# Second expert stage of a two-layer kernel: when its first weights are sent, and from where its first two gathers read

## The chip, the cores and the metric

The kernel runs on one core of a Trainium2 chip. A core has a matrix engine (TensorE, PE in the profile; its weight loads are PEld), a vector engine (VectorE, DVE), a scalar engine (ScalarE, ACT), GpSimd (POOL) and a queue that issues most DMAs (SyncE, SP or SPq). The metric is the device time of one execution in microseconds. The kernel before takes 781.3 us, the median of 3 runs from 780.98 to 781.67.

## The reference

A sequence of 16 meta tokens and 256 tokens of 1024 features goes through two layers. Each has a mixer (layer 0: two recurrences side by side; layer 1: gated linear attention, `gla_mix`, in chunks of 64 tokens) and then 32 experts with a hierarchical router. Everything is f32. The change touches only the second layer's experts and the final norm:

```python
def rms_norm(x, gain):
    y = x * lax.rsqrt(jnp.mean(x * x, axis=-1, keepdims=True) + 1e-6)
    return y * gain

def hier_moe(h, ...):                      # h: 272 x 1024
    g_idx = argmax(h @ w_group + b_group)  # 1 of 4 groups
    # of the 8 experts of that group the 2 with the largest logits,
    # weights: softmax over the two, times the group's probability
    for e in range(32):                    # w_gate, w_up: 1024 x 256, w_down: 256 x 1024
        hid = silu(h @ w_gate[e]) * (h @ w_up[e])
        y = y + (hid @ w_down[e]) * combine[:, e:e + 1]

h = h + gla_mix(rms_norm(h, o_norm) @ o_w_in) @ o_w_out
h = h + hier_moe(rms_norm(h, m_norm[1]), ...)
return rms_norm(h[:, 16:], final_norm)
```

## The kernel before

**Memory.** `M` is one tile of 128 partitions by 45312 floats, used again and again. In the expert stages it holds four slots of 8192 floats (`slots`, 4 MB each), from columns 0, 8192, 16384 and 37120, the normalised rows `xn` (24576 to 27648), the one-hots `R` and weighted one-hots `RW[0]`, `RW[1]`, the gathered tokens `xgT`, and the outputs `yst`. `H` holds the residual rows: `H[:, 0]` and `H[:, 1]` the 256 tokens, `H[:, 2]` the meta tokens, which layer 1's experts don't need any more.

**The expert stage.** `experts(y)` exists once for each engine, y being the layer. Experts go in 8 turns of four, q = 0 to 7, and each turn has three units of weights of 4 MB: unit 3q is gate, 3q + 1 up, 3q + 2 down. `UNIT_SLOT` gives each unit its slot; in layer 1 units 0 to 11 take slots 0, 1, 2, 3 in turn. The first half of a gate or up unit (`0:D`) holds contraction blocks k = 0 to 3, the second (`D:2*D`) k = 4 to 7. SyncE issues the DMAs in the order of units, each behind a wait for the slot's last reader: in layer 1 unit 0 behind `mix_part` 1 (the first of four chunks of the mixer's output, L395), unit 1 behind `mix_part` 4 (L397), unit 3 in two halves behind `res_done` 9 and 11 (the output projection's blocks, L399, L412), unit 4 behind `half_done` 3 (the first half of unit 0's gate is used, L429), unit 5 in halves behind `half_done` 4 and the end of unit 1, and from unit 6 on each behind the end of the unit that had the slot (L433). Unit 4's first half is set aside elsewhere (`set_aside`, semaphore `ld_half`). Unit 6 takes slot 2 after unit 2, the down weights of q = 0.

**A turn on TensorE** (L1576 to L1633): gate (L1554), then `combined` of the turn before (L1512), up (L1554), the weighted one-hots turned back (L1505), the gather for the next turn (L1497, blocks k = 0 to 3), the transposes of hid (L1617), down (L1630), and the rest of the gather (k = 4 to 7). A gather is a matmul for each k and each of two token tiles n, with `xn[:, n, k, :]` (128 adjacent floats) stationary and `R[:, n, :]` moving; `gathered` on VectorE applies the gain `gm`. In q = 0 the gather is `first_gather` (L1411), interleaved with the router's matmuls and the halves of gate and up, so that it goes on while the second tile's tokens are still being routed. Each f32 matmul stands in the trace as two records, each with its weight load.

**Normalisation.** ScalarE squares and sums the rows (L544, L807, L814), VectorE inverts the root (L1990), and ScalarE's `normed(n)` (L803) writes `xn[:, n]`, reading H with a step of 8 floats (`"p (d k) -> p k d"`) and writing adjacent ones, times `rs`. `xn_set` counts these. `first_onehot` and `onehot` on VectorE make `R` from the slot numbers `RM`, `weighted` makes `RW` from `R`; `R_set` and `RW_set` count them. `link` makes an engine wait for its own last instruction.

**The end.** `fnb` is the gain of the final norm spread over all partitions, loaded by a DMA of 0.5 MB into `H[:, 2]` during layer 1's projections (L509, after the group g = 8). The last accumulations, the norm and three output DMAs follow q = 7. `keep_busy` is a filler of matmuls on ones. `oproj` counts the projections of layer 1 (22 in all), `qk_set` the scaled keys and queries of its 6 levels.

## Time and profile before

| | |
|---|---|
| median of 3 runs | 781.3 us (780.98 to 781.67) |
| span of the profiled execution | 778.7 us, mean granted TensorE clock 0.975 |
| PE, DVE, ACT, POOL busy | 92%, 42%, 26%, 4% of the span |
| DMA | 242.14 MB, mean 311 GB/s; 420 to 424 GB/s in the full slices |
| chain that ended last | PE 60%, DMA 15%, DVE 4% |
| second expert stage, from its first weight load to the last output | 522.3 to 778.7 us |

The profile is one execution; its times count from the span's start. The runs' time lies 2.6 us above the span. The page cuts the span into 40 slices of 19.5 us. A timeline row gives start, length, engine, line, operation, what it writes and reads, shapes and, in brackets, the engine's idle time before it and what ended that. Rows of one kind in sequence are merged, with their count.

### The profile page before, as it was taken

How to read it: one execution, taken by the hardware profiler on the slowest of the kernel's cores; microseconds unless marked ns; L12 is line 12 of the kernel's file. 1: busy time of each engine (PE TensorE's matmuls, PEld its weight loads, DVE VectorE, ACT ScalarE, POOL GpSimd, SP SyncE). 2: the span in 40 equal slices, each digit the busy share in tenths (PEclk: the TensorE clock that was granted, in tenths of full speed). 3: DMA queues.
4: the chain of work that ended last, by engine and by line, in shares of the span. 5: the costliest groups of instructions: out<-in, count | busy, mean ns of one | idle time of the engine just before them, and what ended most of it. 6: DMA issues, size and time to landing. Idle time of an engine off the chain costs nothing.

```text
span 778.7 us, 16693 instructions
## 1 busy us (share of the span) xinstructions
PE 718.9 (92%) x7444; PEld 459.4 (59%) x7444; DVE 324.4 (42%) x688; ACT 205.9 (26%) x414; POOL 31.7 (4%) x99
## 2 busy tenths in 40 slices
PE   9999999999989998999999999999998976786696
PEld 7778787658646464564548746884764543343342
DVE  7476977535353422333235065541445321221222
ACT  2574577215100000000041454630510000000003
POOL 7006000000000000000000000000000000000000
PEclk9999999999999997999999999999999998989999
DMA  8644113499999999999999731019999999999995
GB/s 265 201 107 142 56 57 112 161 418 417 386 420 419 420 421 421 417 419 422 411 339 370 231 107 58 2 36 424 421 391 421 422 420 419 421 422 422 420 406 199
DMA packets 72757, 242.14 MB, mean 311 GB/s; under 512 B 9894, under 2 KB 37660, under 8 KB 52588
## 3 DMA queue, kind: packets, MB, share of 16 engines
q1 hardware_dynamic: 72476, 240.52, 79.0%
q8 instruction: 59, 0.97, 0.5%
q10 hardware_dynamic: 208, 0.54, 0.2%
q14 instruction: 14, 0.11, 0.0%
HBM read 240.00 MB, written 1.05 MB: 310 GB/s over the span
## 4 chain that ended last, share of the span: by engine, by line
PE 60%; DMA 15%; DVE 4%; issue 1%; SPq 1%; ACT 0%; ACTq 0%
PE ps L1554 11%; PE ps L1874 10%; PE ps L1396 7%; PE ps L1497 6%; DMA M<-in_m_w_gate_dram 6%; PE ps L1630 5%; PE ps L1512 5%; DMA M<-in_m_w_up_dram 4%; DMA M<-in_m_w_down_dram 4%; PE ps L1035 2%; DVE H L2488 1%; PE ps L1411 1%; PE ps L1696 1%; PE ps L1768 1%; PE ps L1505 1%
## 5 line engine op out<-in xcount | busy, mean ns | idle before, releaser
L1554 PE MATMUL ps<-M 128*32 128x256 f32 x2016 | 124.2, 396 | 18.4 <-DMA M<-in_m_w_gate_dram 11.4
L1554 PEld LDWEIGHTS ps<-M 128*32 128x32 f32 x2016 | 66.7, 114 | 74.7 <-issue 16.9
L1089 PE MATMUL ps<-M 128*128 128x272 f32 x352 | 85.3, 397 | 0.1
L1874 PE MATMUL ps<-M 128*128 128x256 f32 (+2 forms) x288 | 79.9, 434 | 0.0
L1497 PEld LDWEIGHTS ps<-M 128*128 128x128 f32 x608 | 71.5, 192 | 12.3 <-issue 11.8
L1497 PE MATMUL ps<-M 128*128 128x128 f32 x608 | 76.9, 278 | 0.0
L1089 PEld LDWEIGHTS ps<-M 128*128 128x128 f32 x352 | 65.6, 190 | 15.4 <-issue 1.7
L1630 PE MATMUL ps<-M 128*32 128x512 f32 x448 | 58.7, 671 | 15.5 <-DMA M<-in_m_w_down_dram 15.5
L1512 PE MATMUL ps<-M 128*128 128x512 f32 (+1 forms) x120 | 62.8, 647 | 5.3 <-DVE H L2488 5.3
L1874 PEld LDWEIGHTS ps<-M 128*128 128x128 f32 x288 | 53.7, 190 | 22.6 <-issue 15.6
L2485 DVE TENSOR_TENSOR H<-H,ps 128x512 f32<-128x512 f32 x60 | 41.2, 687 | 57.5 <-PE ps L1512 57.3
L1396 PE MATMUL ps<-M 128*128 128x512 f32 (+1 forms) x160 | 57.5, 512 | 0.0
L2464 DVE TENSOR_TENSOR M<-ps,gm 128x512 f32<-128x512 f32 x28 | 19.4, 692 | 59.7 <-PE ps L1497 59.7
L1512 PEld LDWEIGHTS ps<-M 128*128 128x128 f32 (+1 forms) x120 | 19.9, 194 | 40.7 <-DVE H L2485 18.1
L1630 PEld LDWEIGHTS ps<-M 128*32 128x32 f32 x448 | 15.7, 120 | 47.7 <-issue 46.5
L831 ACT ACTIVATE M<-ps 128x256 f32<-128x256 f32 x16 | 6.1, 383 | 140.7 <-PE ps L1554 140.7
L1396 PEld LDWEIGHTS ps<-M 128*128 128x128 f32 x160 | 29.6, 190 | 23.0 <-issue 21.5
L833 ACT ACTIVATE M<-ps 128x272 f32<-128x272 f32 x16 | 6.4, 397 | 127.1 <-PE ps L1505 127.1
L2540 DVE COPY M<-ps 128x512 f32<-128x512 f32 x14 | 9.7, 692 | 64.2 <-PE ps L1630 64.2
L839 ACT ACTIVATE M<-ps 128x512 f32<-128x512 f32 x16 | 9.6, 597 | 62.2 <-PE ps L1630 57.3
L2488 DVE TENSOR_TENSOR H<-H,ps 16x256 f32<-16x256 f32 x32 | 13.3, 414 | 29.7 <-PE ps L1514 29.4
L1021 POOL TENSOR_SCALAR M<-M,rs 128x512 f32<-128x512 f32 x1 | 1.6, 1566 | 548.0 <-DVE rs L1990 548.0
(462 smaller groups left out, 843.6 us busy)
## 6 DMA issues: line engine op xcount, KB each, us to landing
M<-in_m_w_gate_dram SPq DMA_DIRECT2D x31, 2048.0 KB, 19.0
M<-in_m_w_down_dram SPq DMA_DIRECT2D x24, 2048.0 KB, 22.8
M<-in_m_w_up_dram SPq DMA_DIRECT2D x24, 2048.0 KB, 21.6
M<-in_o_w_in_dram SPq DMA_DIRECT2D x12, 1024.0 KB, 9.5
M<-in_e_w_in_dram SPq DMA_DIRECT2D x11, 1024.0 KB, 6.7
M<-in_m_w_down_dram SPq DMA_DIRECT2D x10, 1024.0 KB, 18.1
M<-in_m_w_up_dram SPq DMA_DIRECT2D x9, 1024.0 KB, 17.9
M<-in_m_w_down_dram SPq DMA_DIRECT2D x4, 1536.0 KB, 13.3
```

Source lines behind the costliest of these rows:

```text
L1035: pe.matmul(ps[:, bank, :].rearrange("p (a c) -> p a c", a=4), ones[:, :], ones[:, :].unsqueeze(1).to_broadcast([P, 4, P]), start=True, st ...
L1089: ins = pe.matmul(ps[:, n % 4, 0:T], wringE[:, (n // 2) % 4, k, (n % 2) * P:(n % 2) * P + P], (xnE if n else xuE)[:, k], start=(k == 0), s ...
L1396: ins = pe.matmul(res, mixT[:, k, TOK[n]], w_out, start=(k == 0), stop=(k == 7))
L1497: ins = pe.matmul(ps[:, 1 + k // 4, (k % 4) * P:(k % 4) * P + P], xn[:, n, k, :], R[:, n, :], start=(n == 0), stop=(n == nt - 1))
L1512: return pe.matmul(ps[:, bank, :], rt_[:, TOK[n]], ys[:, 512 * hf:512 * hf + 512], start=True, stop=True)
L1554: ins = pe.matmul(ps[32 * e:32 * e + 32, 3 * x, 0:FF], xgT[q % 2][:, k, 32 * e:32 * e + 32], w, start=(k == 0), stop=(k == KD - 1))
L1630: ins = pe.matmul(ps[r, 4 + hf, :], hidT[:, k, r], dn_w[UNIT_SLOT[y][u]][:, e, k, 512 * hf:512 * hf + 512], start=(k == 0), stop=(k == 1))
L1874: ins = pe.matmul(ps[rows, unit % 4, 0:n], lhs(k), rhs(k), start=(k == 0), stop=(k == KD - 1))
L2464: return tt(xgT[q % 2][:, 4 * b:4 * b + 4], ps[:, 1 + b, :].rearrange("p (k t) -> p k t", k=4), gm[:, y, 4 * b:4 * b + 4].unsqueeze(2).to_ ...
L2485: return tt(H[:, n, c], H[:, n, c], ps[:, 6 + j % 2, :], ALU.add)
L2488: ins = tt(H[0:META, 2, c], H[0:META, 2, c], ps[32 * g:32 * g + META, 6 + j % 2, 0:256], ALU.add)
L2540: v.tensor_copy(yst[q % 2][:, 512:1024], ps[:, 5, :]).then_inc(s("yd"), 1)
```

## The change

**Loads.** In layer 1, unit 0 is sent when the projections are done (`oproj` 22) instead of with `mix_part` 1: its experts 2 and 3 whole, and of experts 0 and 1 the second half. Their first halves go where `xn[:, 0:2]` lies, after `mix_part` 4. The room left in slot 0 takes the second halves of unit 4's experts 0 and 1 at once. Unit 1's experts 0 and 1 are sent behind `qk_set` 6, the rest behind `mix_part` 4. Half an expert's down weights of unit 5 are loaded into `H[:, 2]` during the projections.

**Gathers.** In layer 1 the gathers for q = 0 and q = 1 read `H` itself with a step of 8 floats (`rows_at`), and the factor `rs` goes into the one-hot: `first_onehot` and `onehot(1)` write the plain one-hot into `RW[0]` and `RW[1]` and multiply it into `R`. `normed(0)` and `normed(1)` come in q = 0, before the silu and after the copy of hidT, and VectorE's first accumulation waits for them, since it changes `H`.

**Final norm.** The gain is loaded as 8 rows of 128 into `before`. At the head of q = 4 and q = 5 TensorE spreads four rows each over all partitions into PSUM bank 3, and ScalarE copies them to `fnb`, now at column 26624. Up of that turn waits for the copy.

Cut to its core (`...` marks what is left out):

```diff
-        fnb = H[:, 2, :]
+        first_half = [[], [xn[:, n].rearrange("p k t -> p (k t)") for n in range(2)]]
+        fnb = at(26624, D)
+        fn_rows = before[0:KD, :]
+        down_half = H[:, 2, :]
...
                         if y == 0:
                             sp.wait_ge(s("oc_set"), NC)
                         else:
-                            sp.wait_ge(s("mix_part"), 1)
+                            sp.wait_ge(s("oproj"), sum(O_UNITS))
+                            sp.dma_start(slots[j][:, 2:4, :], gate[:, 2:4, :]).then_inc(s(f"ld_s{j}"), 16)
+                            sp.dma_start(slots[j][:, 0:2, D:2 * D], gate[:, 0:2, D:2 * D]).then_inc(s(f"ld_s{j}"), 16)
+                            sp.dma_start(slots[j][:, 0:2, 0:D], up[:, 4:6, D:2 * D]).then_inc(s("ld_half"), 16)
+                            continue
                     elif u == 1 and y == 1:
+                        sp.wait_ge(s("qk_set"), 6)
+                        sp.dma_start(slots[j][:, 0:2, :], up[:, 0:2, :]).then_inc(s(f"ld_s{j}"), 16)
                         sp.wait_ge(s("mix_part"), 4)
+                        sp.dma_start(xn[:, 0:2].rearrange("p n k t -> p n (k t)"), gate[:, 0:2, 0:D]).then_inc(s("ld_s0"), 16)
+                        sp.dma_start(slots[j][:, 2:4, :], up[:, 2:4, :]).then_inc(s(f"ld_s{j}"), 16)
+                        continue
...
                         elif u == 4:
-                            sp.dma_start(slots[j][:, 2 * h:2 * h + 2, 0:D], src[:, 4 + 2 * h:6 + 2 * h, D:2 * D]) \
-                                .then_inc(s(f"ld_s{j}"), 16)
+                            if h == 1:
+                                sp.dma_start(slots[j][:, 2:4, 0:D], src[:, 6:8, D:2 * D]).then_inc(s(f"ld_s{j}"), 16)
                         elif u == 5:
                             if h == 1:
                                 wait_through(UNIT_PREV[y][u])
-                            sp.dma_start(slots[j][:, :, D * h:D * h + D], src[:, 4:8, D * h:D * h + D]).then_inc(s(f"ld_s{j}"), 16)
+                            sp.dma_start(slots[j][:, 1 - h:4, D * h:D * h + D], src[:, 5 - h:8, D * h:D * h + D]).then_inc(s(f"ld_s{j}"), 16)
...
                 if g == 8:
-                    sp.dma_start(fnb, a["final_norm"].rearrange("(o d) -> o d", o=1).broadcast_to([P, D])).then_inc(s("ld_wr"), 16)
+                    sp.dma_start(fn_rows, a["final_norm"].rearrange("(k c) -> k c", c=P)).then_inc(s("ld_gn"), 16)
+                    sp.dma_start(down_half, a["m_w_down"][1, 4].rearrange("(p k) d -> p (k d)", k=2)[:, 0:D]).then_inc(s("ld_wr"), 16)
...
-                act.wait_ge(s("rec"), (5, 10)[y])
-                normed(0)
-                if nt == 3:
+                if y == 0:
+                    act.wait_ge(s("rec"), (5, 10)[y])
+                    normed(0)
                     normed(2)
...
-                act.wait_ge(s("rec"), (6, 11)[y])
-                normed(1)
+                if y == 0:
+                    act.wait_ge(s("rec"), (6, 11)[y])
+                    normed(1)
...
                 for q in range(NQ):
                     n = NQ * y + q
+                    if q == 0 and y == 1:
+                        act.wait_ge(s("half_done"), 2 * y + 1)
+                        act.wait_ge(s("rec"), (6, 11)[y])
+                        normed(0)
+                    if y == 1 and q in (4, 5):
+                        act.wait_ge(s("vec_tr"), q + 3)
+                        nc.scalar.activation(fnb[:, 512 * q - 2048:512 * q - 1536], ps[:, 3, :], ACT.Copy).then_inc(s("rb_set"), 1)
...
+                    if q == 0 and y == 1:
+                        normed(1)
...
+            def rows_at(n, k):
+                return H[:, n, :].rearrange("p (d k) -> p k d", k=KD)[:, k, :]
...
-                        ins = pe.matmul(ps[:, GATHER_BANK[k // 2], (k % 2) * P:(k % 2) * P + P], xn[:, n, k, :], R[:, n, :],
+                        ins = pe.matmul(ps[:, GATHER_BANK[k // 2], (k % 2) * P:(k % 2) * P + P], rows_at(n, k) if y == 1 else xn[:, n, k, :], R[:, n, :],
...
-                pe.wait_ge(s("xn_set"), (2, 4)[y])
+                if y == 0:
+                    pe.wait_ge(s("xn_set"), (2, 4)[y])
...
-                            ins = pe.matmul(ps[:, 1 + k // 4, (k % 4) * P:(k % 4) * P + P], xn[:, n, k, :], R[:, n, :],
+                            from_rows = rows_at(n, k) if first and y == 1 else xn[:, n, k, :]
+                            ins = pe.matmul(ps[:, 1 + k // 4, (k % 4) * P:(k % 4) * P + P], from_rows, R[:, n, :],
...
+                            elif u == 0 and k < KD // 2 and e < len(first_half[y]):
+                                w = first_half[y][e][:, FF * k:FF * k + FF]
...
+                    if y == 1 and q in (4, 5):
+                        pe.wait_ge(s("ld_gn"), 80)
+                        for k in range(4 * q - 16, 4 * q - 12):
+                            ins = pe.matmul(ps[:, 3, (k % 4) * P:(k % 4) * P + P], ident[0:KD, k:k + 1].to_broadcast([KD, P]), fn_rows,
+                                            start=True, stop=True)
+                        ins.then_inc(s("vec_tr"), 1)
...
+                            if y == 1 and q in (4, 5):
+                                pe.wait_ge(s("rb_set"), q + 3)
                             half_gu(3 * q + 1, q, 1, range(4 if q == 0 and y == 1 else 0, KD))
...
-                        gather(ks=range(0, 2))
+                        if y == 1 and q == 1:
+                            pe.wait_ge(s("xn_set"), (3, 5)[y])
+                        gather(ks=range(0, 2), first=(q == 0))
...
-                        gather(s("g_done"), range(2, 4))
+                        gather(s("g_done"), range(2, 4), q == 0)
...
-                                ins = pe.matmul(ps[r, 4 + hf, :], hidT[:, k, r],
-                                                dn_w[UNIT_SLOT[y][u]][:, e, k, 512 * hf:512 * hf + 512], start=(k == 0), stop=(k == 1))
+                                w = dn_w[UNIT_SLOT[y][u]][:, e, k, 512 * hf:512 * hf + 512]
+                                if y == 1 and u == 5 and e == 0 and k == 0:
+                                    w = down_half[:, 512 * hf:512 * hf + 512]
+                                ins = pe.matmul(ps[r, 4 + hf, :], hidT[:, k, r], w, start=(k == 0), stop=(k == 1))
                         ins.then_inc(s("dn_done"), 1)
-                    gather(ks=range(4, KD)).then_inc(s("g_done"), 1)
+                    gather(ks=range(4, KD), first=(q == 0)).then_inc(s("g_done"), 1)
...
+                    if y == 0:
+                        return tt(R[:, t_].rearrange("p t (e c) -> p t e c", e=4),
+                                  iota[:, 1:CAP + 1].unsqueeze(1).unsqueeze(1).to_broadcast([P, m, 4, CAP]),
+                                  RM[:, t_, 0:4].unsqueeze(3).to_broadcast([P, m, 4, CAP]), ALU.is_equal).then_inc(s("R_set"), 1)
+                    link(tt(RW[0][:, t_].rearrange("p t (e c) -> p t e c", e=4),
+                            iota[:, 1:CAP + 1].unsqueeze(1).unsqueeze(1).to_broadcast([P, m, 4, CAP]),
+                            RM[:, t_, 0:4].unsqueeze(3).to_broadcast([P, m, 4, CAP]), ALU.is_equal))
+                    tt(R[:, t_], RW[0][:, t_], wide3(rs[:, ri], P, t_, m), ALU.mult).then_inc(s("R_set"), 1)
...
+                    hot = RW[q] if y == 1 and q == 1 else R
+                    made = tt(by_slot(hot), iota[:, 1:CAP + 1].unsqueeze(1).unsqueeze(1).to_broadcast([P, nt, 4, CAP]),
+                              RM[:, t_, 4 * q:4 * q + 4].unsqueeze(3).to_broadcast([P, nt, 4, CAP]), ALU.is_equal)
+                    if hot is not R:
+                        link(made)
+                        made = tt(R[:, t_], hot[:, t_], wide3(rs[:, ri], P), ALU.mult)
+                    made.then_inc(s("R_set"), 1)
                     v.wait_ge(s("R_set"), (NQ + 1) * y + q + 2)
...
-                    tt(by_slot(RW[q % 2]), by_slot(R), WT[:, t_, 4 * q:4 * q + 4].unsqueeze(3).to_broadcast([P, nt, 4, CAP]),
+                    tt(by_slot(RW[q % 2]), by_slot(RW[q] if y == 1 and q < 2 else R), WT[:, t_, 4 * q:4 * q + 4].unsqueeze(3).to_broadcast([P, nt, 4, CAP]),
...
+                    if y == 1 and q == 0:
+                        v.wait_ge(s("xn_set"), (3, 5)[y])
...
-                    v.wait_ge(s("ld_wr"), 176)
+                    v.wait_ge(s("rb_set"), 8)
```

## Rows read from the trace of the kernel before

**Rows 1.** The page: share and rate of the DMA engines in 40 slices.
```profile
DMA  8644113499999999999999731019999999999995
GB/s 265 201 107 142 56 57 112 161 418 417 386 420 419 420 421 421 417 419 422 411 339 370 231 107 58 2 36 424 421 391 421 422 420 419 421 422 422 420 406 199
```

**Rows 2.** Timeline of PE, 604 to 779 us: start, length, engine, line, operation, idle before.
```profile
621.47 2.05 PE L1497 MATMUL ps<-M 128*128 128x128 f32 x16
627.12 5.35 PE L1554 MATMUL ps<-M 128*32 128x256 f32 x64 [3.60 <-DMA M<-in_m_w_gate_dram]
...
656.93 5.35 PE L1554 MATMUL ps<-M 128*32 128x256 f32 x64 [2.52 <-DMA M<-in_m_w_gate_dram]
```

**Rows 3.** The chain of work that ended last, in order of time: start, length.
```profile
737.97 6.27 PE ps L1630 x32
```

**Rows 4.** Timeline of the SyncE queue: when it issued the weight loads.
```profile
522.30 0.88 SPq L468 DMA_DIRECT2D M<-in_m_w_gate_dram  x2
529.24 0.88 SPq L468 DMA_DIRECT2D M<-in_m_w_up_dram  x2
...
568.08 0.88 SPq L461 DMA_DIRECT2D M<-in_m_w_up_dram  x2
...
580.87 0.88 SPq L468 DMA_DIRECT2D M<-in_m_w_gate_dram  x2
586.44 0.88 SPq L468 DMA_DIRECT2D M<-in_m_w_up_dram  x2
```

**Rows 5.** DMA issues, windows 522:523 and 580:582 us: KB each, median us to landing.
```profile
M<-in_m_w_gate_dram SPq DMA_DIRECT2D x2, 2048.0 KB, 10.5
...
M<-in_m_w_gate_dram SPq DMA_DIRECT2D x2, 2048.0 KB, 13.7
```

**Rows 6.** Timeline of PE, 511 to 582 us.
```profile
511.73 1.89 PE L1874 MATMUL ps<-M 128*128 128x256 f32 x8
...
552.02 1.87 PE L1431 MATMUL ps<-wrc,M 128*128 128x36 f32 x16
...
560.76 1.58 PE L1411 MATMUL ps<-M 128*128 128x128 f32 x12
...
564.00 1.93 PE L1411 MATMUL ps<-M 128*128 128x128 f32 x12
566.09 3.66 PE L1554 MATMUL ps<-M 128*32 128x256 f32 x64 [0.16 <-DVE M L2469]
569.68 1.16 PE L1411 MATMUL ps<-M 128*128 128x128 f32 x8
...
575.05 1.06 PE L1497 MATMUL ps<-M 128*128 128x128 f32 x8
...
577.17 3.64 PE L1630 MATMUL ps<-M 128*32 128x512 f32 x32
```

**Rows 7.** Timeline of DVE, 560 to 574 us: the first one-hots and the second.
```profile
560.33 0.29 DVE L2405 TENSOR_TENSOR M<-iota,M 128x128 f32<-128x128 f32 x1
...
564.37 0.29 DVE L2405 TENSOR_TENSOR M<-iota,M 128x128 f32<-128x128 f32 x1
...
573.64 0.43 DVE L2455 TENSOR_TENSOR M<-iota,M 128x256 f32<-128x256 f32 x1
```

**Rows 8.** Lines 803 and 544 (ACT): shortest/median/longest in ns, first and last start.
```profile
L803 ACT ACTIVATE M<-H,rs x5: 2135/2157/2160, 180.2 to 560.1; 128x1024 f32<-128x1024 f32 x5
...
L544 ACT ACTIVATE M<-H x5: 1042/1050/1057, 5.4 to 548.4; 128x1024 bf16<-128x1024 f32 x4, 16x1024 bf16<-16x1024 f32 x1
```

**Rows 9.** Timeline of ACT in q = 0: the silu.
```profile
572.91 0.38 ACT L831 ACTIVATE M<-ps 128x256 f32<-128x256 f32 x1 [3.86 <-PE ps L1554]
```

**Rows 10.** Timeline of PE's weight loads, the first gather of tile 0.
```profile
560.74 1.41 PEld L1411 LDWEIGHTS ps<-M 128*128 128x128 f32 x12 [0.20 <-issue]
```

**Rows 11.** Lines 1617 (step of 2 floats) and 1505 (adjacent): weight loads, in ns.
```profile
L1617 PEld LDWEIGHTS ps<-ident,M x32: 194/199/218, 204.0 to 761.7; 128*128 128x128 f32 x32
...
L1505 PEld LDWEIGHTS ps<-ident,M x32: 186/190/192, 574.5 to 761.3; 128*128 128x128 f32 x32
```

More of the change, by code:

```diff
@@ L1529, in loaded @@
                     j = UNIT_SLOT[y][u]
-                    pe.wait_ge(s(f"ld_s{j}"), 32 * (FIRST_LAYER[j] * y + UNIT_TURN[y][u] + 1))
+                    more = 0
+                    if (y, u) == (1, 0):
+                        more += 16
+                    pe.wait_ge(s(f"ld_s{j}"), 32 * (FIRST_LAYER[j] * y + UNIT_TURN[y][u] + 1) + more)
                     if y == 0 and u == 1:
```

16 lines of the change are left out of this document (7 added, 9 removed).

## The prediction, made before the changed kernel was run

> **What bounds the kernel now.** I read the page first, for the stage that matters. The DMA engines move about 420 GB/s, all they give here, through nearly every slice of the second expert stage, and fall to 2 and 36 GB/s in the two slices before it [rows 1]. The change works on that border, so the time is in the chain behind it. The PE timeline shows that from the fourth turn of the stage (q = 3) TensorE stands and waits for weights: 3.60 us before gate at 627.12, 2.52 us at 656.93 [rows 2]. A unit of 4 MB takes (656.93 − 627.12)/3 = 9.94 us. The last such wait ends at 737.97; behind it comes only TensorE's own tail, whose first piece took 6.27 us [rows 3]. So the end moves with the stream of weights, one for one.
>
> The stream goes by the SyncE queue, in order. It starts at 522.30. Unit 4 is issued at 568.08, when half of unit 0's gate is used up. Unit 6 is the one that matters. It is issued at 580.87, when the down matmuls of q = 0 (577.17 + 3.64) have ended and slot 2 is free [rows 4, 6]. With an empty queue two loads of 2 MB land 10.5 us after their issue (median, 522.30); unit 6's land after 13.7 us [rows 5]. So 3.2 us of older work stood ahead of unit 6. That is the reserve: **the stream can move forward by 3.2 us at most, unless TensorE ends q = 0 sooner.** Behind it each slot comes free well before the stream wants it: unit 7 is issued at 586.44, and its data flow only when unit 6 has landed, at 627.12 − 3 × 9.94 = 597.3 [rows 2, 4]; the distance grows with each later unit. Nothing later holds the stream.
>
> **Part 1, earlier loads.** Unit 0, a quarter of unit 4 and half of unit 1 no longer wait for the first mixed chunk (522.30) but for the end of the projections, 511.73 + 1.89 = 513.6 [rows 4, 6]: 8.7 us sooner. They are 6 MB, 15 us of stream, to 529 or 530, where the wait for the fourth chunk ends (529.24) [rows 4]. The 0.5 MB of down for unit 5 that comes during the projections, in the place of the norm's broadcast of 0.5 MB, takes 1.2 us more out. Taken alone that is near 9 us. It is lost: the stream then runs dry before 547 to 559, where the output matmuls free slot 3, and again before units 4 and 5, which are still released by TensorE inside q = 0, and stands empty when unit 6 comes. What is left is the 3.2 us, less any delay of q = 0. The issues themselves take 0.4 us of SyncE each, under the stream.
>
> **Part 2, normalisation on ScalarE.** Two passes of 2.16 us leave the way to the router. TensorE did not wait for them: the gathers of tile 0 began at 560.76 and those of tile 1 at 564.8, each just behind its one-hot of VectorE (560.33 + 0.29 = 560.62, 564.37 + 0.29 = 564.66) [rows 6, 7], and the second pass had ended at 560.1 + 2.16 = 562.3 [rows 8]. Gain 0. They come back in q = 0: normed(0) where ScalarE idles 3.86 us before the silu [rows 9], normed(1) beside the down matmuls. Cost 0; without this cover 2.2 us. VectorE's new wait in accumulated(0) has the accumulations and the table of q = 1 behind it, and is met some 7 us early (normed(1) ends near 580, the first combine near 587).
>
> **Part 3, scaled one-hots.** Each first_onehot gets a linked multiplication of 128 columns, as long as the comparison, 0.29 us, and about 0.04 us for the link; onehot(1) one of 256 columns, 0.43 us [rows 7]. The first lies on the path (+0.3 us). The second lies on it too (+0.3 us) if the gathers cost what they did, and is hidden if they become slower; the third has TensorE's turn_back and first gather beside it. Together +0.3 to +0.7 us.
>
> **Part 4, gathers from the residual rows.** This decides. The stationary operand was xn[:, n, k, :], 128 adjacent floats; now it is H with a step of 8 floats, 32 bytes. There are 16 such matmuls in the first gather and 16 in the second, each of two records. The instructions are as many as before; the question is how long a weight load takes. Two rows say that the load is the limit even now: 12 records in 1.41 us, (1.41 − 0.19)/11 = 0.11 us apart, where 0.19 us is one load alone, and the logits with a moving side of only 36 columns are no faster: 1.87 us for 16, about 0.11 us each [rows 6, 10]. Nothing hides a longer load.
>
> No row shows a weight load with this step. Bounds from the nearest: ScalarE reads the same rows of H with the same step of 8 in 2157 ns (L803) and adjacent ones in 1050 ns (L544): +1.08 ns per element, +138 ns for 128 [rows 8]. The weight load of hid with a step of 2 took 199 ns against 190 ns for adjacent ones [rows 11], +9 ns: the lower end, and a load may even be free of any cost (0). Zero stands for a TensorE that does not mind the step. I take **+0.12 us a record**: ScalarE's row is the only one with this very step and these very rows, less a little, since part of its difference may be the f32 output.
>
> The Trainium skill bears both ways. "Advanced Engine Details and Errata", section SBUF Cachelines, has lines of 16 bytes and wants two hits in a line for full rate; ScalarE's 2157 against 1050 ns agrees. By it the 199 ns of step 2 mean (110 + 9)/64 = 1.86 ns a line, and step 8 an estimated 128 × 1.86 = 238 ns against 110, +0.13 us: the sum below with half a microsecond more. "TensorE: Matmul & The Clock Gate", section LDWEIGHTS, gives the load as columns/1.2 ns, 107 ns, with no word on the step; the 0.11 us above agrees, and by that rule alone the load would not change and the first rival would hold.
>
> **The sum.** Ahead of the end of q = 0's down stand 12 + 4 + 16 records of the first gather and 16 of the second [rows 6]: 48 × 0.12 = 5.8 us. Add 0.3 for the first multiplication. Take off the short waits of TensorE in this stretch that are now filled (0.11 before 564.80, 0.16 before 566.09, 0.5 before 570.91): −0.7. So unit 6 is issued 5.4 us later, at 586.3, to an empty queue, and lands 5.4 − 3.2 = 2.2 us later than before. The last 16 strided records follow q = 0's down, and TensorE reaches q = 3 at 623.52 [rows 2] + 5.4 + 1.9 = 630.8 against weights at 629.3; the 1.5 us are made good at once, since gate took 5.35 us behind a wait and takes 3.66 us without one [rows 2, 6], and up waits for its weights anyway. End: **+2.2 us**, span 778.7 + 2.2 = 780.9. The median of the runs is 2.6 us above the span, which I keep: 783.5.
>
> **Part 5, final norm by TensorE.** Four matmuls of 128 columns ahead of gate in q = 4 and q = 5, about 0.9 us each time, and a copy of 0.6 us on ScalarE. TensorE waits 2.52 us for weights at that very place [rows 2]: 0. Without the cover 1.8 us. The wait on rb_set before up has gate's 3.66 us ahead of it: 0. The last stage waits for rb_set where it waited for the old load, both done by then.
>
> **Rivals.** (a) *The step is free for TensorE.* Then only part 3 delays q = 0, +0.7 us, and the stream gains 3.2 − 0.7 = 2.5 us: 778.8. For it: the load with step 2 is almost as fast, and no row shows TensorE suffer from a step. Against: ScalarE's row, and that the load already sets the pace. It decides if the extra is under 0.03 us a record. This is the case on the other side. (b) *The step costs 0.03 to 0.08 us*: 48 of them less the covers give 1.2 to 3.4 us of delay, −1.8 to +0.7, mostly within 0.2%: about 781. (c) *The earlier start reaches the end*, −9 us, 772: it needs unit 6 issued before 575, and that issue belongs to TensorE. I give it nothing but the edge. (d) *The tail*: down at 737.97 took 6.27 us, where the same matmuls took 3.64 us in q = 0 [rows 3, 6]. A shift of the whole stage can put it elsewhere: −2 to +1 us in any case. It widens the range and has no chance of its own.
>
> **How the numbers follow.** Forecast 0.58, with +0.09 to +0.14 us a record: +0.8 to +3.2 us, 782.1 to 784.5, and 1 more for the tail. Rival (a) 0.31, (b) 0.10, (c) 0.01. About 0.2% (1.6 us) is what a measurement of this kernel can tell from no change. Slower: 0.50 of the forecast and 0.02 of (b). Same: 0.08 of the forecast, 0.04 of (a), 0.06 of (b). Faster: 0.27 of (a), 0.02 of (b), 0.01 of (c). The range must hold both sides: from 778.2, just below (a), to 785.2. The forecast's own is 781.8 to 785.2.
>
> **What would show it.** The weight loads of first_gather with about 315 ns where they had 190 (right) or still 190 (rival a). Unit 6 issued near 586 (right) or 581.5 (a). The DMA engines idle just before unit 6: in both. No wait of TensorE for gate at q = 3. The wait for weights before gate at q = 4 and 5 shorter by 0.9 us, its end unmoved by it. Wrong would be the whole reasoning if unit 6 still found older loads ahead of it, or if the first gathers began later than 561.2 for another reason.

## The result, and the profile of the changed kernel

| | before | changed |
|---|---|---|
| median of the runs compared | 781.3 us (779.88 to 783.17, 5 runs) | 788.8 us (785.47 to 789.97, 5 runs) |
| ratio, 95% interval | 1 | 1.0081 (1.0061 to 1.0100) |
| the same again, in a later series | 781.43 us (23 runs) | 786.15 us (785.40 to 787.59, 6 runs); 1.0061 (1.0041 to 1.0081) |
| span of the profiled execution | 778.7 us | 783.7 us, granted clock 0.972 |

The change costs 0.6 to 0.8%. All 11 runs of the changed kernel together have a median of 787.3 us, 5.9 above the 781.4 of before. The prediction said slower by 2.2 us, range 778.2 to 785.2; the direction was right, the size was not.

The page's DMA rows of the changed kernel, in the same 40 slices as [rows 1]:

```profile
DMA  8644113499999999999999531079869999999995
GB/s 262 201 109 139 55 57 110 186 417 415 387 420 419 419 422 421 418 420 421 406 339 370 173 108 56 2 289 385 345 238 379 421 420 420 421 420 421 421 405 196
```

The empty slice ahead of the stage is filled (36 became 289 GB/s), and the rate falls behind it: 385, 345 and 238 where [rows 1] has 424, 421 and 391. The stream was moved forward and then stood.

The queue of SyncE, 512 to 592 us (start, length, what it issued), against [rows 4]:

```profile
513.63 0.37 SPq L399 DMA_DIRECT2D M<-in_m_w_gate_dram  x1
...
530.61 0.37 SPq L407 DMA_DIRECT2D M<-in_m_w_gate_dram  x1
531.02 0.47 SPq L408 DMA_DIRECT2D M<-in_m_w_up_dram  x1
...
572.69 0.37 SPq L474 DMA_DIRECT2D M<-in_m_w_up_dram  x1
574.42 6.06 SPq L478 DMA_DIRECT2D M<-in_m_w_down_dram  x2
588.34 0.88 SPq L480 DMA_DIRECT2D M<-in_m_w_gate_dram  x2
```

Unit 0 leaves 8.7 us sooner. But SyncE's wait for the fourth mixed chunk (`mix_part` 4; called the fourth chunk's wait below, its end being the issue behind it) ends at 530.61 instead of 529.24, unit 4 is released at 572.69 instead of 568.08, and unit 6 at 588.34 instead of 580.87: 7.47 us later. It meets a queue that is all but empty (107 GB/s from 588 to 590 us) and takes 10.5 us to land, where [rows 5] has 13.7.

PE, 518 to 593 us, against [rows 6] (start, length, line, shapes, in brackets the idle time before and what ended it):

```profile
520.31 0.42 PE L1974 MATMUL ps<-M,ones 128*32 128x64 f32 x12
521.84 0.31 PE L1974 MATMUL ps<-M,ones 128*32 128x64 f32 x4 [1.11 <-issue]
...
562.44 3.24 PE L1437 MATMUL ps<-M,H 128*128 128x128 f32 x12 [0.42 <-DVE M L2460]
565.48 2.14 PE L1058 MATMUL ps<-ones 128*128 128x512 f32 x4
...
567.56 3.21 PE L1437 MATMUL ps<-M,H 128*128 128x128 f32 x12
570.69 3.66 PE L1589 MATMUL ps<-M 128*32 128x256 f32 x64
574.28 2.17 PE L1437 MATMUL ps<-M,H 128*128 128x128 f32 x8
...
580.53 2.07 PE L1525 MATMUL ps<-M,H 128*128 128x128 f32 x8
...
584.64 3.64 PE L1679 MATMUL ps<-M 128*32 128x512 f32 x32
588.21 4.08 PE L1525 MATMUL ps<-M,H 128*128 128x128 f32 x16
```

The gathers of 12 and 8 records take about twice what they took. And there is a stall of 1.11 us in the mixer, at 520.73, that no row of before has; the trace puts it down to issue, that is, to nothing that it shows. The weight loads of the strided gathers (shortest/median/longest in ns; `ps<-M,H` are those of layer 1, `ps<-M` the adjacent ones of layer 0):

```profile
L1437 PEld LDWEIGHTS ps<-M x48: 186/192/192, 187.6 to 196.0; 128*128 128x128 f32 x48
L1437 PEld LDWEIGHTS ps<-M,H x32: 312/336/338, 562.4 to 575.9; 128*128 128x128 f32 x32
...
L1525 PEld LDWEIGHTS ps<-M,H x32: 312/335/338, 580.4 to 591.8; 128*128 128x128 f32 x32
```

PE, 652 to 743 us, the waits for weights, against [rows 2, 3], and the spreading of the final norm (L1619):

```profile
652.06 4.94 PE L1679 MATMUL ps<-M 128*32 128x512 f32 x32 [3.70 <-DMA M<-in_m_w_down_dram]
...
658.91 1.15 PE L1619 MATMUL ps<-before,ident 8*128 8x128 f32 x8
661.91 5.15 PE L1589 MATMUL ps<-M 128*32 128x256 f32 x64 [1.85 <-DMA M<-in_m_w_gate_dram]
...
742.98 5.34 PE L1679 MATMUL ps<-M 128*32 128x512 f32 x32 [3.68 <-DMA M<-in_m_w_down_dram]
```

Gate of q = 4 gets its weights at 661.91 instead of 656.93, and the last down at 742.98 instead of 737.97: 5.0 us each, as the span. The last down takes 5.34 us instead of 6.27, but the end is no sooner for it.

One measure helps in all that follows. The data of unit 11 (down of q = 3) end a wait of TensorE in every profile, at 647.09 before and 652.06 after; from there to the end of the span are 131.5 to 131.8 us in before, the changed kernel and the first four experiments alike. So **the end is unit 6's issue, plus the time until the data of unit 11 are there (six units of 4 MB, 6 to 11), plus a constant**: the middle term is 66.22 us before (580.87 to 647.09) and 63.72 after. The 2.5 us between the two are all that the stream gains, and 7.47 − 2.5 = 5.0.

### The profile page after: what moved, and what is told of

The parts are those of the page before. It is cut to its first block, busy times and chain, and to the rows that moved or that the text cites. A ratio compares the mean times of both kernels' runs of the same rounds, so it can differ in the third digit from the quotient of the medians.

```text
span 783.7 us, 16735 instructions
## 1 busy us (share of the span) xinstructions
PE 729.4 (93%) x7460; PEld 469.0 (60%) x7460; DVE 325.2 (42%) x691; ACT 206.7 (26%) x416; POOL 31.5 (4%) x99
## 4 chain that ended last, share of the span: by engine, by line
PE 59%; DMA 13%; DVE 4%; SPq 4%; issue 1%; ACT 0%; PEld 0%; PEldq 0%; ACTq 0%
PE ps L1589 11%; PE ps L1922 10%; DMA M<-in_m_w_gate_dram 7%; PE ps L1419 7%; PE ps L1525 7%; DMA M<-in_m_w_down_dram 5%; PE ps L1540 5%; PE ps L1679 4%; SPq L470 2%; PE ps L1437 2%; DVE H L2546 1%; PE ps L1058 1%; SPq L464 1%; PE ps L1816 1%; PE ps L1533 1%
## 5 line engine op out<-in xcount | busy, mean ns | idle before, releaser
L1589 PEld LDWEIGHTS ps<-M 128*32 128x32 f32 x2016 | 65.5, 114 | 67.2 <-issue 15.9
L1525 PEld LDWEIGHTS ps<-M 128*128 128x128 f32 x576 | 68.5, 194 | 11.4 <-issue 10.9
L1112 PEld LDWEIGHTS ps<-M 128*128 128x128 f32 x352 | 65.6, 190 | 15.5 <-issue 1.7
L1525 PE MATMUL ps<-M 128*128 128x128 f32 x576 | 73.6, 280 | 0.0
L1922 PEld LDWEIGHTS ps<-M 128*128 128x128 f32 x288 | 53.7, 190 | 22.6 <-issue 15.6
L1679 PEld LDWEIGHTS ps<-M 128*32 128x32 f32 x444 | 15.2, 120 | 47.2 <-issue 46.1
L1419 PEld LDWEIGHTS ps<-M 128*128 128x128 f32 x160 | 29.6, 190 | 23.0 <-issue 21.5
```

Source lines behind the costliest of these rows:

```text
L1112: ins = pe.matmul(ps[:, n % 4, 0:T], wringE[:, (n // 2) % 4, k, (n % 2) * P:(n % 2) * P + P], (xnE if n else xuE)[:, k], start=(k == 0), s ...
L1419: ins = pe.matmul(res, mixT[:, k, TOK[n]], w_out, start=(k == 0), stop=(k == 7))
L1525: ins = pe.matmul(ps[:, 1 + k // 4, (k % 4) * P:(k % 4) * P + P], from_rows, R[:, n, :], start=(n == 0), stop=(n == nt - 1))
L1589: ins = pe.matmul(ps[32 * e:32 * e + 32, 3 * x, 0:FF], xgT[q % 2][:, k, 32 * e:32 * e + 32], w, start=(k == 0), stop=(k == KD - 1))
L1679: ins = pe.matmul(ps[r, 4 + hf, :], hidT[:, k, r], w, start=(k == 0), stop=(k == 1))
L1922: ins = pe.matmul(ps[rows, unit % 4, 0:n], lhs(k), rhs(k), start=(k == 0), stop=(k == KD - 1))
```

## The experiments

The first four pull the two large parts of the change apart. They ran together (before: 781.45 us, 35 runs).

**1. The gathers read adjacent floats.** The features come in another order, so the output is another; instructions, bytes and waits are the same.

```diff
             def rows_at(n, k):
-                return H[:, n, :].rearrange("p (d k) -> p k d", k=KD)[:, k, :]
+                return H[:, n, k * P:(k + 1) * P]
```

> The changed kernel, but the first two gathers read 128 adjacent floats of H instead of every eighth. (So the features of the gathered tokens are in another order than the weights' rows, and the experts' output of q = 0 and 1 is another one; amount and order of work are the same.) Theory A, the step of 8 floats is what costs: the weight loads of the gathers fall from 336 to 192 ns, q = 0's down ends 48 x 0.144 = 6.9 us sooner than in the changed kernel, near 581.4 to 582 in its profile, unit 6 meets an empty queue and lands about 1 us sooner than in the kernel before; time 780 us, plus whatever the early loads cost in stalls (1 to 4 us): 780 to 784. Theory B, the earlier traffic or the moved passes of ScalarE are what costs and the step only adds what would be hidden: no more than 2 us are won, 787 us. Theory C, the whole loss is the step: 778.8, as the first rival of the prediction had it.

Measured: 781.83 us (779.11 to 783.93, 12 runs), ratio 0.9993 (0.9974 to 1.0012): within theory A's range, B and C are out. Unit 6 is issued at 582.96, 52.23 us behind the fourth chunk's wait instead of 57.73. That is 1 us later than theory A had it, and the queue was not empty: unit 6 took 12.0 us to land.

**2. The late start.** The early loads wait for the first mixed chunk again; the step stays.

```diff
-                            sp.wait_ge(s("oproj"), sum(O_UNITS))
+                            sp.wait_ge(s("mix_part"), 1)
...
-                        sp.wait_ge(s("qk_set"), 6)
```

> The changed kernel with one part undone: unit 0 and the first half of unit 1 wait again for the mixer's first and fourth chunk. Theory A: the queue is empty at unit 6 anyway, so nothing of the early start is lost, and the stall of 1.1 us in TensorE's issue at 520.7, which came when 6 MB of weights ran beside the mixer's end, goes: q = 0's down ends at 586.9 instead of 588.3, time 1.4 us below the changed kernel's if the stall is the same in each run, 2 to 4 us below if its other runs (spans 785.8 to 788.2 against 783.7 of the profiled one) have longer ones: 784 to 787. Theory D, the early start is worth its 3 us of reserve: 2 to 3 us slower than the changed kernel, 791.

Measured: 786.38 us (783.98 to 791.06, 12 runs), ratio 1.0057 (1.0038 to 1.0075). Unit 6 at 588.65, landing 10.4 us later. Without the early start the kernel is no slower than the changed one; theory D's 791 did not come. The stall is gone in this profile, but unit 6 is no sooner: the filler took 3.01 us instead of 2.14, at a granted clock of 0.50 (1.2 GHz) from 564 to 566 us.

**3. Both edits together.**

> Both edits of the two runs before at once: adjacent reads (another order of features, same amount of work) and the late start. What is left of the change is the scaled one-hots, normed in q = 0, the weights in xn's place, the 0.5 MB of down during the projections, and the final norm by TensorE. Theory A: q = 0's down ends at 581.5 (0.7 us late by the multiplications), the stream has 1.2 us less before unit 6, which lands 1.2 us sooner: 780 us, 1 us below the kernel before or the same. Theory B (moved passes of ScalarE cost): over 783.

Measured: 781.6 us (779.37 to 783.86, 12 runs), ratio 0.9998 (0.9980 to 1.0016). Unit 6 comes 53.89 us behind the fourth chunk's wait, 1.66 more than in experiment 1 with the same gathers. The granted clock was 0.50 from 564 to 566 us here and 1.00 there: the first twelve records took 2.07 instead of 1.60 us, the filler 3.14 instead of 1.88.

**4. The kernel before with the early start alone** (unit 0 at the end of the projections, unit 1's first half behind `qk_set` 6).

> The kernel before with one part added: unit 0 whole at the end of the projections and the first half of unit 1 behind the last keys; nothing else. Theory A: the stream before unit 6 is done early, unit 6 lands 581 + 13.2 = 594.3 instead of 597.3 if q = 0 is not delayed, 1.4 us less gain with a stall of TensorE's issue near 520: 778.4 to 780. If the runs of the changed kernel that lie 2 to 4 us above its profiled one do so by such stalls, this one shows it as well: a spread over 3 us in its runs, median 780 to 782. Theory D: -3 us, 778.3, with no stall.

Measured: 782.7 us (781.22 to 785.33, 12 runs), ratio 1.0011 (0.9996 to 1.0026). Unit 6 at 582.31, 1.44 later than before; 1.0 of that is a stall in the mixer (below). Unit 11's data come 66.18 us behind it: of the reserve nothing is used.

What follows from the four: the step accounts for nearly the whole loss (with it 786.4 to 787.3, without it 781.6 to 781.8, whatever the start). The early start is worth nothing in either company: 9 us of stream moved ahead are lost before unit 6. Nor do these medians show a price of it that is clear of the noise: what it costs the mixer is read from the profiles alone.

The next four ran together (before: 781.43 us, 23 runs).

**5. The changed kernel again,** unaltered.

> The changed kernel, nothing altered, beside the others and with a profile of its own. It settles how much of the gap between the median (+7.5 us) and the profiled execution (+5.0 us) is spread. Theory A (the profiled execution was simply a fast one): the median comes out 786 to 789, and this profile shows TensorE's stall ahead of the stage of another length than 1.11 us, with unit 6 issued 57 to 58.5 us behind the last mixed chunk as before. Rival: the median falls to about 784.5, 1.75 us above the span of 783.7 plus the usual 1 us; then 2 to 4 us of the first result were chance of one job.

Measured: 786.15 us (785.40 to 787.59, 6 runs), 2.7 us below the first median. Its profile has the same span, 783.6, unit 6 at 588.20, and the stall again, shorter:

```profile
520.92 0.42 PE L1974 MATMUL ps<-M,ones 128*32 128x64 f32 x12
522.04 0.30 PE L1974 MATMUL ps<-M,ones 128*32 128x64 f32 x4 [0.70 <-issue]
```

So of the first result's 7.5 us, 4.7 come back, and all eleven runs give 5.9. The granted clock was 0.969 to 0.973 in the first five runs and 0.970 to 0.979 in these six; whether that made the difference, no run tells.

**6. The changed kernel without the filler** between the first gather of tile 0 and the ranks of tile 1.

```diff
                 first_gather(y, range(0, 6), (0, 2)[0:2 - y])
-                if y == 1:
-                    keep_busy(2, 3)
```

> The changed kernel without the two filler matmuls (keep_busy(2, 3)) between the first gather of tile 0 and the ranks of tile 1. They took 2.14 us there, and VectorE's input to the ranks (A_set) was ready before they began, since the strided gather ended 1.7 us later than before. Theory A (everything ahead of the down matmuls of q = 0 is on the path one for one): TensorE ends q = 0 some 1.9 to 2.1 us sooner, unit 6 is issued so much sooner, and the end comes 1.9 us sooner than in the unchanged kernel of this job, about 785.5 to 786. Rival B (something else waits behind it, such as VectorE's second one-hot or a lower clock without the filler): at most 0.5 us, and the idle time of TensorE before the ranks or before the second gather grows by what the filler took.

Measured: 784.23 us (782.60 to 786.71, 12 runs), ratio 1.0030 (1.0015 to 1.0045), 1.9 us below experiment 5. Unit 6 comes 55.68 us behind the fourth chunk's wait (588.30 − 532.62) instead of 57.39 to 57.73. As theory A said. The VectorE row of the changed kernel shows how it came to lie on the path: the ranks' input was written by 565.3, and then VectorE stood for TensorE:

```profile
565.05 0.25 DVE L2437 SCALAR_TENSOR_TENSOR M<-M 128x32 bf16<-128x32 f32 x1
...
567.70 0.19 DVE L2446 SCALAR_TENSOR_TENSOR M<-ps,M 128x32 f32<-128x32 f32 x1 [2.24 <-PE ps L1516]
```

In the kernel before, the filler covered a wait of TensorE (experiment 12 shows 0.55 us of it with half the filler). The slower gather in front of it used up that wait, and the filler kept its length: the 1.7 us that the first twelve loads cost would have been hidden, had the filler given way.

**7. The kernel before with half an expert of unit 5 loaded early and the norm spread by TensorE** (`fnb`, `fn_rows`, `down_half` and what belongs to them in the diff; nothing of the gathers, one-hots or early start).

> The kernel before with only two pieces of the change: half an expert's down weights of unit 5 (0.5 MB) loaded into the meta tokens' rows during the projections in the place of the norm's broadcast, and the final norm spread by TensorE in q = 4 and q = 5. The step, the early start and the scaled one-hots are left out. Theory A (what moves the stream is only how little stands ahead of unit 6, and 0.5 MB is 1.2 us of it): unit 6 is issued at the same time as before, lands about 1.2 us sooner (reserve was 2.5 to 3.2 us), and the whole end moves by 1.2 us: 780.2, ratio 0.9985. TensorE's four small matmuls ahead of gate lie in its wait for weights: 0. Rival B (the spreading costs, or the reserve is not reached by work taken out of unit 5): 781.4 or more, ratio 1.000 or above, and the wait for weights before gate of q = 4 ends no sooner than before.

Measured: 780.58 us (779.65 to 786.06, 12 runs), ratio 0.9991 (0.9974 to 1.0007). The interval holds no change and theory A's 0.9985 both. In the profile unit 11's data came 65.95 us behind unit 6's issue instead of 66.22: a gain of 0.3 us, not 1.2. The half megabyte is gone (the load is shown with 1536 KB), but the DMA engines moved 354 GB/s from 576 to 578 us where before they moved 397. Why is open.

**8. The step as a scale.** First gather of layer 1 with steps of 1 to 8 floats, a line for each (the tokens of q = 0 hold other features):

```diff
-                        ins = pe.matmul(..., rows_at(n, k) if y == 1 else xn[:, n, k, :], ...)
...
+                        elif k == 0:
+                            ins = pe.matmul(out_, H[:, n, 0:128:1], R[:, n, :], ...)
+                        elif k == 1:
+                            ins = pe.matmul(out_, H[:, n, 0:255:2], R[:, n, :], ...)
...
+                        elif k == 7:
+                            ins = pe.matmul(out_, H[:, n, 0:1017:8], R[:, n, :], ...)
```

> The changed kernel, where the first gather of layer 1 reads its eight feature blocks from the residual rows with steps of 1, 2, 3, 4, 5, 6, 7 and 8 floats, a line of its own for each, so that each step's weight load has its own row. The tokens gathered for q = 0 hold other features than the reference wants. It measures the cost of the step. Theory A (cost by lines of 16 bytes, as ScalarE's read suggests: one line for each element from a step of 4 on): 190 ns at step 1, rising in proportion up to step 4, and level at about 335 ns from 4 to 8. Theory B (cost by bytes spanned): a straight line from 190 at step 1 to 336 at step 8, with 199 at step 2 and 250 at step 4. Theory C (32 bytes are special, and below them the load is nearly free): 190 to 210 ns for steps 1 to 7 and 336 at 8 alone.

It ran once, in 785.1 us, and its time is not compared. Weight loads of 128 x 128 f32 with steps of 1, 2, 3, 4, 5 and 8 floats, in this order (shortest/median/longest in ns):

```profile
L1441 PEld LDWEIGHTS ps<-M,H x4: 186/188/189, 562.5 to 568.9; 128*128 128x128 f32 x4
L1443 PEld LDWEIGHTS ps<-M,H x4: 196/197/198, 562.8 to 569.1; 128*128 128x128 f32 x4
L1445 PEld LDWEIGHTS ps<-M,H x4: 254/258/263, 563.0 to 569.4; 128*128 128x128 f32 x4
L1447 PEld LDWEIGHTS ps<-M,H x4: 317/324/330, 563.3 to 569.8; 128*128 128x128 f32 x4
L1449 PEld LDWEIGHTS ps<-M,H x4: 295/316/319, 563.8 to 574.0; 128*128 128x128 f32 x4
...
L1455 PEld LDWEIGHTS ps<-M,H x4: 334/335/336, 568.2 to 575.4; 128*128 128x128 f32 x4
```

Theory A, with one correction: step 2 is almost free (197), step 3 costs +70, step 4 already +136, and 5 to 8 add nothing much (316 to 335). The Trainium skill, "Advanced Engine Details and Errata", section SBUF Cachelines, has lines of 16 bytes that must be hit twice for full rate; the trace agrees: two floats of a line are the last step that is free, and from one float a line on the price is level. Theories B and C are out.

The last four ran together (before: 781.43 us, 35 runs).

**9. One megabyte early.** The kernel before; expert 0 of gate at the end of the projections, the other three with the first mixed chunk.

```diff
+                            sp.wait_ge(s("oproj"), sum(O_UNITS))
+                            sp.dma_start(slots[j][:, 0:1, :], gate[:, 0:1, :]).then_inc(s(f"ld_s{j}"), 16)
                             sp.wait_ge(s("mix_part"), 1)
+                            sp.dma_start(slots[j][:, 1:4, :], gate[:, 1:4, :]).then_inc(s(f"ld_s{j}"), 16)
+                            continue
```

> The kernel before, with 1 MB of unit 0 (expert 0 of gate) sent at the end of the projections and the other 3 MB with the first mixed chunk, as before. The early traffic then fills only 2.5 us, 514.3 to about 517, and is over when TensorE reaches the place (near 520.5 us) where it stalled 0.5 to 1.1 us in every kernel with 6 MB sent early and in none without. Theory A (the stall comes from weights in flight at that moment): no stall, the fourth mixed chunk is ready as early as before (issue of unit 1 near 529.1), unit 6 issued at 581, and the time is the one before, 781.4 within 0.6. Rival B (the stall comes from the order of the issues, or from SyncE's waits, whatever is in flight): the stall stays, 0.5 us or more, and the time is near that of the early start alone, 782.5.

Measured: 781.62 us (780.46 to 787.41, 12 runs), ratio 1.0010 (0.9992 to 1.0028), and no stall; the 16 records stand in one piece:

```profile
520.26 0.43 PE L1930 MATMUL ps<-M,ones 128*32 128x64 f32 x16
520.63 1.15 PE L1918 MATMUL ps<-M 128*64 128x64 f32 x32
```

The time from the end of the projections to the end of the fourth chunk's wait, in all profiles:

| kernel | early loads | that time, us | stall shown, us |
|---|---|---|---|
| before | none | 15.62 | none |
| 2, 3, 7, 11, 12 | none | 15.62 to 15.63 | none |
| 9 | 1 MB | 15.59 | none |
| changed | 6 MB | 16.98 | 1.11 |
| changed again (5) | 6 MB | 16.58 | 0.70 |
| 1 | 6 MB | 16.39 | 0.52 |
| 4 | 6 MB | 16.63 | 0.77 |
| 6 | 6 MB | 16.81 | 0.94 |
| 8 | 6 MB | 16.53 | 0.65 |
| 10 | 6 MB | 16.48 | 0.60 |

The early traffic costs the mixer 0.8 to 1.4 us, always at the same instruction (behind the twelfth record of that group), and only if weights are in flight then. That fixed place would fit a fetch of instructions that comes late behind the weights: the DMA rows have a packet of 0.02 MB of an instruction queue about 5 to 6 us behind the end of the projections in the seven profiles with a stall (519 to 520 us in the changed kernel), and 1 to 3 us sooner where nothing stalls (516 to 517 us in before, 517 to 518 in experiment 9). No run shows that TensorE waited for it, so how the traffic stalls TensorE stays open; that it does is shown.

**10. The step in the first gather only.** The gather for q = 1 reads adjacent floats (its tokens hold other features).

```diff
-                            from_rows = rows_at(n, k) if first and y == 1 else xn[:, n, k, :]
+                            from_rows = H[:, n, k * P:(k + 1) * P] if first and y == 1 else xn[:, n, k, :]
```

> The changed kernel, with the step of 8 floats only in the first gather; the gather for q = 1 reads adjacent floats of the residual rows. Its features come in another order, so the tokens of q = 1 are not what the reference wants. 32 of the 48 strided records ahead of the end of q = 0 are left, and none behind it. Theory A (each strided record on the path costs the same 0.12 us, and the stream follows TensorE one for one): the down matmuls of q = 0 start 2.0 us sooner, unit 6 is issued 2.0 us sooner (55.7 us behind the last mixed chunk), and the end comes 2 us sooner than in the unchanged changed kernel, about 785. Rival B (only the records ahead of the first gate count, since gate and up hide the later ones): nothing, about 787.

Measured: 785.18 us (783.21 to 786.63, 12 runs), ratio 1.0040 (1.0026 to 1.0054), 1.0 below experiment 5 and 2.1 below the eleven runs of the changed kernel. Unit 6 comes 56.22 us behind the fourth chunk's wait, 1.2 to 1.5 sooner; the filler took 2.65 us in this profile instead of 1.88 in experiment 5's, which makes up the rest of the 2.0. So at unit 6's issue the price goes by the record, wherever it stands, and rival B is out. At the end less of it is left. Unit 6 took longer to land than the 10.4 and 10.5 us of experiment 5 and the changed kernel:

```profile
M<-in_m_w_gate_dram SPq DMA_DIRECT2D x2, 2048.0 KB, 12.2
```

The last load of unit 5 is released by TensorE too, at the end of up of q = 0. The gather for q = 1 lies between that release and unit 6's; once it is short, unit 6 is issued 5.9 us behind unit 5's last load instead of 7.9 and finds more of it still on its way (it lands some 3.9 us behind unit 6's issue, 1.3 in the changed kernel). At unit 11's data only 0.1 to 0.5 us of the gain are left in this profile (120.92 us behind the fourth chunk's wait, against 121.05 and 121.45), and the 1.0 us between the medians of experiments 10 and 5 is not clear of their spread. Sixteen of 48 records fewer give back a fifth of the loss by experiment 5 and a third by all eleven runs; the runs can't tell which.

**11. Adjacent features, late start, and one filler matmul in the place of two.** **12. Experiment 7 with one filler matmul.** Both change the one line below on top of their kernels; 11 has the features in another order.

```diff
-                    keep_busy(2, 3)
+                    keep_busy(1, 3)
```

> Adjacent features and the late start as before in this study, and one filler matmul in the place of two ahead of the ranks of tile 1. With two, the filler took 3.14 us at a low granted clock and ended 2.0 us after VectorE's input was ready; the order of the features is not the reference's. Theory A (the filler was on the path, and one is enough): unit 6 is issued 52 us behind the last mixed chunk instead of 53.9, the stream gains the 1.9 us, and the time is 779.7 to 780, ratio 0.998, whatever the clock in 560 to 566 does. Rival B (the shorter filler lets the clock fall further on into the first gathers and gate): some matmuls behind it take twice their time, unit 6 comes no sooner than with two, 781.6 or more.

> The kernel before with half an expert's down weights in the meta tokens' rows and the norm spread by TensorE, and one filler matmul in the place of two. The profile of it with two fillers had the ranks' input ready 0.4 us before the filler ended. Theory A: q = 0 ends 0.3 to 0.4 us sooner, and with the half megabyte less ahead of unit 6 the time is 780.2, ratio 0.9985. Rival B (the clock falls without the second filler, or something else is late there): TensorE stands before the ranks and q = 0 ends no sooner, 780.6 or above.

Measured: 11: 781.49 us (778.98 to 784.01, 12 runs), ratio 0.9999 (0.9982 to 1.0016). 12: 780.97 us (779.79 to 784.36, 12 runs), ratio 0.9983 (0.9964 to 1.0002). In the profile of 11 unit 6 comes 51.98 us behind the fourth chunk's wait, 1.9 sooner than in experiment 3, as theory A had it. Most of that is the clock and not the filler: the granted clock was 1.00 from 560 to 570 us here and 0.83 in experiment 3, and experiment 1, with two filler matmuls at 1.00, has 52.23. So the second matmul costs 0.25 us at full clock, and TensorE waits 0.45 us for VectorE behind the shorter filler:

```profile
562.93 1.02 PE L1057 MATMUL ps<-ones 128*128 128x512 f32 x2
564.40 0.19 PE L1426 MATMUL ps<-M,ones_h 128*128 128x32 bf16 x1 [0.45 <-DVE M L2436]
```

Its span is 777.2 us, 1.5 below before's. But that execution took 778.98 us, the fastest of the twelve, and their median is before's. So the gain isn't proven, and whether one filler matmul keeps the clock up, a single profile can't show. In the profile of 12 unit 6 comes 51.50 us behind the fourth chunk's wait, where experiment 7 has 51.64: TensorE waits 0.55 us for VectorE in the place of the second matmul. Neither 11 nor 12 beats the kernel before by more than the measurement can tell.

## Why the prediction was right or wrong

**What bounds the kernel: right.** The end followed the stream one for one (5.0 us at unit 11, at gate of q = 4, at the last down and in the span), and the stream followed unit 6, which TensorE releases.

**The reserve: right in kind, too large in size.** The prediction took 13.7 − 10.5 = 3.2 us from the landing of unit 6. Its landing time did fall to 10.5, but at unit 11 only 66.22 − 63.72 = 2.5 us were left of it. It also holds in experiment 2, without any early start (63.67), and experiment 4 with the early start alone has 66.18: the loads sent at 513.6 use nothing of the reserve, since they run ahead of releases in the middle of q = 0 that they can't pass. The 1.5 MB taken out of units 4 and 5 used some 1.6 us of it (64.51, 64.66 and 64.70 in experiments 1, 3 and 10; 63.92 in experiment 11, which this doesn't explain). The rest came only where the slow gather for q = 1 put 7.9 us between unit 5's last load and unit 6 (63.60 to 63.72 in five profiles). The prediction let unit 6's release alone bound the end; unit 5's last load, released by TensorE a little earlier, bounds it as well.

**Part 1, earlier loads: right that they bring nothing, wrong that they cost nothing.** They were costed at the reserve as a gain and at 0.4 us of SyncE "under the stream". Not asked was what 6 MB in flight do to an engine that computes at the same time in stretches where the DMA engines were idle before. They cost TensorE 0.8 to 1.4 us in the mixer, 1.37 in the profile of the changed kernel (the row with 1.11 us of issue). This is the first missing term. The prediction had named its sign, first gathers later than 561.2 for another reason; they began at 562.44, 1.37 us of it for this and 0.31 for the multiplication. No row of before could size it; a bound on both sides, as the unknown load time got, would have been due.

**Part 2, normalisation: right.** `normed(0)` took 2.15 us from 573.79 and `normed(1)` 2.17 from 583.14, both beside TensorE, and no engine waited for them.

**Part 3, the one-hots: right.** The multiplication takes 0.29 us, and the first gather starts 31.83 us behind the fourth chunk's wait instead of 31.52: +0.31.

**Part 4, the step: right in kind and nearly in size.** Predicted +0.12 us a record, and weight loads of about 315 ns; measured 336 against 192 ns. Between the gathers' first record and the down matmuls lie 22.20 us instead of 16.41: +5.79, where the prediction had 5.8 − 0.7 = 5.1. A group of 8 took 2.07 instead of 1.06 us, so a record costs 0.126: 48 of them are 6.1, less 0.6 for the short waits, which went nearly as predicted (0.7), plus 0.26 for the filler, which took 2.14 instead of 1.88 us at a granted clock of 0.83 in 560 to 570 us. The choice of ScalarE's row over the load with step 2 was what made the direction right, and experiment 8 shows why the step of 2 was no neighbour of a step of 8: 197 ns at a step of 2, 324 at a step of 4 already.

What the part missed is the filler. It was kept as a term that doesn't change, and the sum had the first 12 records on the path in full. They were, but only because the filler stood behind them; experiment 6 gives 1.9 us back without it. Part 4's term of 5.1 us was thus too small by 0.7 and, in its first third, avoidable.

**Part 5, final norm: right.** The spreading took 1.15 us (0.9 predicted) in a wait of TensorE, which shrank from 2.52 to 1.85 us at q = 4 and from 2.73 to 1.48 at q = 5, and the weights ended the wait both times.

**The sum.** Predicted 5.4 − 3.2 = 2.2 us. Profiled 7.47 − 2.5 = 5.0. The 2.8 between are 1.4 (the stall), 0.7 (the gathers) and 0.7 (the reserve). **The step that failed** is first Part 1's, which put at nothing what the early loads cost TensorE, where the profile shows 1.4 us; the other two are terms that were mis-sized: the delay by the gathers, 5.8 us and not 5.1, and the reserve, 2.5 us and not 3.2. Of the further distance to the medians, 0.9 is there over all 11 runs (5.9 us), and 1.6 more in the first five runs didn't come back; the cause of both stays open. The predicted time of 783.5 also rested on a gap of 2.6 us between span and median; the profiled execution of the changed kernel was itself the fastest of its five.

**The rivals.** (a), the step is free, has fallen with the 336 ns. What it gave for the case without the step, a gain of 2.5 us, did not come either (experiment 1: no change). There unit 6 was issued 2.1 us later than before: 0.8 by the stall, 0.6 by the two multiplications ahead of tile 0's and tile 1's gather, and 0.7 in the part of the program ahead of the change; the way to unit 11 was only 1.7 us shorter (64.51), since unit 5's last load still stood ahead of unit 6. (c), the early start reaches the end, had no support: experiment 4. The tail, (d), moved by 0.9 us within its stage and by nothing in the end.

## What to carry to other kernels

A step in the stationary operand has a price that its neighbour doesn't tell. Here a weight load of 128 x 128 f32 took 197 ns at a step of two floats against 188 for adjacent ones, but 316 to 335 ns from a step of four on, and where the load sets the pace of short matmuls (0.24 us a record instead of 0.11) that lies on the path in full. Sending loads sooner helps only up to the next load that a compute engine releases; look for all of those first, and ask what the early traffic does to the engines that run beside it. A filler that covered a wait turns into work on the path as soon as something in front of it becomes longer, so each one on the way has to be checked against when its successor's input is ready.

## What the runs showed of the hardware that was not expected

- With 6 MB of weights in flight TensorE stood 0.5 to 1.1 us at one place of the mixer, with issue as the cause, in all seven profiles, and not with 1 MB or none.
- Weight loads of 128 x 128 f32 took 188, 197, 258, 324, 316 and 335 ns with steps of 1, 2, 3, 4, 5 and 8 floats.
- The granted clock in 560 to 570 us was 1.00 in some kernels and 0.83 in others with nearly the same work there (0.50, the level of 1.2 GHz, from 563 to 566 us in the changed kernel; TensorE had been busy 2.74 of the 3 us from 558 us on there, and 2.85 in experiment 5, which kept 1.00); four records of the filler took 1.88 us at the one and up to 3.14 us at the other (experiment 3), while they were on the path. Between experiments 1 and 3 that alone moved unit 6's issue by 1.66 us.
- Runs of one kernel spread by 2 to 7 us here, ten times what some of the steps in this study are worth; a single profiled execution of experiment 11, 1.5 us faster than before's, had a median that was no faster.
